# First units of a stage in two halves of 256 tokens, and the second mixer's values ahead of its keys and queries, in a kernel of two transformer blocks

## What is computed

```python
def token_mixing(x, mem, positions, w_in, b_in, pool_w, pool_scale, w_mem_kv, w_br, w_out):
    proj = jnp.einsum('bsd,de->bse', x, w_in) + b_in
    u_pool, q, k, v, iq, ik, iw, mq, gate_logits = jnp.split(proj, split_points, axis=-1)
    branches = (pool_branch(u_pool, pool_w, pool_scale),
                dsa_branch(q, k, v, iq, ik, iw, positions),   # rotary on q, k, iq, ik; top-128 by index score
                memory_branch(mq, mem, w_mem_kv))
    ...
def dsa_branch(...):
    rel = jax.nn.relu(jnp.einsum('bqhd,bsd->bqhs', iqb, ik) * (IDX_HEAD_DIM ** -0.5))
    score = jnp.einsum('bqhs,bqh->bqs', rel, iwb)
    ...
def second_block(...):
    for l in range(DEPTH):
        mix = token_mixing(...)
        x = layer_norm_2(DN_ALPHA_2 * x + mix, ln1_g[l], ln1_b[l])
        ffn = moe(...)                                        # 16 experts, two for each token
        x = layer_norm_2(DN_ALPHA_2 * x + ffn, ln2_g[l], ln2_b[l])
```

## Time and profile before

| | us |
|---|---|
| median of 3 runs | 3320.78 |
| lowest, highest | 3319.87, 3322.07 |
| profiled execution | 3319.54 |
| its span | 3317.7 |

### The profile page before, as it was taken

One profiled execution on the slowest core, in us unless ns is written; L12 is line 12 of the kernel. 1 busy time (PEld: TensorE's weight loads), 2 busy tenths in 40 slices (PEclk: granted clock), 3 DMA queues, 4 the chain that ended last, 5 costly groups with the idle time before them and its releaser, 6 DMA issues.

```text
span 3317.7 us, 44936 instructions
## 1 busy us (share of the span) xinstructions
PE 2972.4 (90%) x13284; PEld 2350.1 (71%) x13284; DVE 1805.6 (54%) x2681; ACT 1417.1 (43%) x2009; POOL 1100.6 (33%) x663
## 2 busy tenths in 40 slices
PE   5898999999879999999999977997599999969993
PEld 4666788876657888766777856885458777748883
DVE  3775444036655341346544157996556533169996
ACT  3525455225353552211344126885111443228882
POOL 2212344542122445444743521111336543601101
PEclk8998999999989999998999988998789999979996
DMA  3212233432122334322321337997212322349993
GB/s 111 64 32 83 76 95 95 166 91 67 33 71 81 96 95 153 109 71 58 101 67 48 105 141 289 411 411 283 79 58 82 88 64 64 111 161 401 411 410 132
DMA packets 373732, 461.46 MB, mean 139 GB/s; under 512 B 33396, under 2 KB 280262, under 8 KB 373512
## 3 DMA queue, kind: packets, MB, share of 16 engines
q1 hardware_dynamic: 353664, 392.05, 35.0%
q0 software_dynamic: 14976, 54.53, 4.3%
q10 hardware_dynamic: 4872, 12.26, 1.1%
HBM read 423.10 MB, written 35.65 MB: 138 GB/s over the span
## 4 chain that ended last, share of the span: by engine, by line
PE 48%; issue 33%; POOL 11%; DVE 5%; ACT 1%; DMA 1%; POOLq 0%; SPq 0%; DVEq 0%; ACTq 0%
POOL unit_lo L407 9%; PE bank L487 7%; PE bank L488 6%; PE bank L1997 4%; PE bank L2132 3%; PE bank L2133 3%; PE bank L2136 3%; PE bank L759 2%; PE bank L2146 2%; PE bank L2147 2%; PE bank L2150 2%; PE bank L2058 1%; PE bank L493 1%; PE bank L2074 1%; PE bank L494 1%
## 5 line engine op out<-in xcount | busy, mean ns | idle before, releaser
L407 POOL TENSOR_TENSOR unit_lo<-unit_raw,unit_hi 128x1024 fp32r<-128x1024 f32 (+1 forms) x176 | 422.5, 2402 | 893.0 <-ACT unit_hi L400 893.0
L487 PE MATMUL bank<-xT_hi,unit_hi 128*128 128x512 f32 x1680 | 692.3, 412 | 22.5 <-DVE xT_lo L661 9.9
L488 PE MATMUL bank<-xT_lo,unit_hi 128*128 128x512 f32 x1680 | 664.9, 396 | 0.0
L487 PEld LDWEIGHTS bank<-xT_hi,unit_hi 128*128 128x128 f32 x1680 | 322.4, 192 | 121.6 <-issue 44.6
L488 PEld LDWEIGHTS bank<-xT_lo,unit_hi 128*128 128x128 f32 x1680 | 322.1, 192 | 71.0 <-issue 7.7
L392 POOL TENSOR_TENSOR unit_lo<-unit_raw,unit_hi 128x1024 fp32r<-128x1024 f32 (+3 forms) x172 | 354.1, 2059 | 14.4
L400 ACT ACTIVATE unit_hi<-unit_raw 128x1024 fp32r<-128x1024 f32 (+1 forms) x176 | 184.9, 1052 | 406.6 <-PE bank L759 175.6
L390 POOL TENSOR_SCALAR unit_hi<-unit_raw 128x1024 fp32r<-128x1024 f32 (+3 forms) x172 | 159.6, 928 | 589.2 <-PE bank L1997 296.8
L759 PE MATMUL bank<-xT_hi,unit_lo 128*128 128x512 f32 x1040 | 256.9, 389 | 0.0
L472 DVE TENSOR_TENSOR wt_lo<-wt,wt_hi 128x1024 fp32r<-128x1024 f32 x192 | 229.2, 1222 | 32.1 <-ACT wt_hi L467 31.3
L472 DVE TENSOR_TENSOR xT_lo<-wt,xT_hi 128x1024 fp32r<-128x1024 f32 x192 | 234.5, 1223 | 12.3 <-ACT xT_hi L467 2.3
(11 more groups left out here) (514 smaller groups left out, 6471.4 us busy)
## 6 DMA issues: line engine op xcount, KB each, us to landing
wt<-in_w SPq DMA_DIRECT2D x384, 512.0 KB, 8.5
unit_raw<-in_w_in SPq DMA_DIRECT2D x276, 256.0 KB, 3.1
unit_raw<-in_w_ffn_up SPq DMA_DIRECT2D x176, 256.0 KB, 3.2
unit_raw<-in_w_ffn_down SPq DMA_DIRECT2D x88, 256.0 KB, 3.1
unit_raw<-in_w_out SPq DMA_DIRECT2D x64, 256.0 KB, 2.8
y_rows<-yb POOLq DMA_DIRECT2D x32, 512.0 KB, 7.3
y_rows<-zeros POOLq DMA_DIRECT2D x24, 512.0 KB, 5.2
unit_raw<-in_w_br SPq DMA_DIRECT2D x96, 128.0 KB, 2.2
```

The lines of the kernel that those rows point to most:

```text
L407: pool.eng.tensor_tensor(lo, raw, hi.bitcast(F32), SUB).then_inc(self.split, 1)
L487: pe.matmul(out, wh, xh, start=first, stop=False)
L488: pe.matmul(out, wh, xl, start=False, stop=False)
```

## The change

1. `norm_pe` is gone. `turned_rows` turns one tile. In `rows_products` tile i - 1 is turned behind the products of tile i; only the last tile is left for later.
2. `begun_units` starts the next stage: when tiles 0 and 1 have their low halves, the first unit is multiplied with 256 tokens (`first_half`); then the last tile is turned; then the second unit's first half; and when all low halves are there, the second halves of both. It stands at the start of the first and second block's layers and of the feed-forward part. The router's products are cut in two in the same way. To begin a layer, the last tile of the stage before is turned inside the next layer (hence the count 6 of `norm_tr`), and once more at the very end of the program.
3. DVE forms a tile's low half one tile later, between the variance and the inverse of the next but one; ACT alternates roots and copies.
4. In the second mixer the four value units come directly behind the index weights, tiles in the order 2, 3, 0, 1. DVE adds the value bias, loaded to all partitions, while it evicts them. Index scores are single: nine within the value units, the other fifteen before and behind units 5 to 12, over two banks. The memory rows are turned behind unit 15.

```diff
+        def first_half(T, j, half):
+            c = slice(half * 2 * P, half * 2 * P + 2 * P)
+            wh, wl = (w[j % SPLIT][:].rearrange("p (k c) -> p k c", c=P) for w in (ring.hi, ring.lo))
+            o = bank[j % SPLIT][:, c]
+            T.eng.wait_ge(ring.hi_made, ring.hi_is(T, j))
+            for k in range(KC):
+                two_of_three(T.eng, o, wh[:, k, :], xT_hi[:, k, c], xT_lo[:, k, c], k == 0)
+            T.eng.wait_ge(ring.split, ring.split_is(T, j))
+            for k in range(KC):
+                last = T.eng.matmul(o, wl[:, k, :], xT_hi[:, k, c], start=False, stop=k == KC - 1)
+            if half:
+                last.then_inc(ring.done, 1)
+        def begun_units(T, tile, first):
+            T.eng.wait_ge(norm_lo.sem, norm_lo.at(T, 2 * tile + 4))
+            first_half(T, first, 0)
+            turned_rows(T, tile + NT - 1)
+            first_half(T, first + 1, 0)
+            T.eng.wait_ge(norm_lo.sem, T.alone(norm_lo.at(T, 2 * (tile + NT))))
+            first_half(T, first, 1)
+            first_half(T, first + 1, 1)
...
# norm_v
-                    if i == NT - 1:
-                        low(0)
+                    if 0 < i < NT - 1:
+                        low(i - 1)
                     inverse(i)
                     finished(i)
-                for i in range(1, NT):
-                    low(i)
+                low(NT - 2)
+                low(NT - 1)
...
# rows_products
+                if i:
+                    turned_rows(T, tile + i - 1)
...
# tensor1, feed-forward part
-            norm_pe(T, 0)
-            T.eng.wait_ge(norm_lo.sem, T.alone(norm_lo.at(T, 8)))
-            with pe.Fori(0, FC // 2) as i:
+            begun_units(T, 0, U_UP)
+            for s in (2, 3):
+                chunk(T, ring, U_UP + s, bank[s])
+            T.eng.wait_ge(up_lo.sem, T.alone(up_lo.at(T, 1)))
+            with pe.Fori(1, FC // 2) as i:
...
# tensor2, the values
+            for j in range(4):
+                wh, wl = ring.weights(T, U2_V + j)
+                for x, i in enumerate(V_ORDER):
+                    if j == 0 and i < 2:
+                        T.eng.wait_ge(proj_ev.sem, proj_ev.at(T, 4 + i))
+                    for kk in range(2):
+                        k, cs, n = 2 * j + kk, slice(i * P, i * P + P), slice(kk * S, kk * S + S)
+                        last = triple(pe, bank[i][:], xT_hi[:, k, cs], xT_lo[:, k, cs], wh[:, n], wl[:, n], k == 0, k == 7)
+                    if x == NT - 1:
+                        last.then_inc(ring.done, 1)
+                    if j == 0 and x % 2:
+                        swap(3 + x // 2)
+                    elif j and x < NT - 1:
+                        index_score()
...
-                        pe.matmul(bank[i][:], ones[0:1, :], brow[:, 0:S], start=True, stop=False)
...
+            for c in range(5, 21):
+                if c < 8:
+                    T.eng.wait_ge(gv_ev.sem, gv_ev.at(T, c - 4))
+                else:
                     T.eng.wait_ge(proj_ev.sem, proj_ev.at(T, c - 2))
+                if c < ROPED:
+                    index_score()
                 chunk(T, ring, V_CH[c], bank[c % 3])
+                if 7 <= c < ROPED + 2:
+                    swap(c - 2)
+                if c < ROPED - 1:
+                    index_score()
+                if c == ROPED + 2:
+                    memory_turned()
...
# scalar2
-            act.dma_start(brow[:, 0:S], t["b_in_2"][bass.ds(l, 1), C_V:C_V + S]).then_inc(pl.sem, pl.up(A))
+            act.dma_start(v_bias, over(t["b_in_2"][bass.ds(l, 1), C_V:C_V + S], [P, S])).then_inc(pl.sem, pl.up(A))
...
# vector2
+            V.eng.wait_ge(ring.done, ring.products(V, U2_V + 3))
+            for i in (2, 0, 1, 3):
+                v.tensor_tensor(vv[:, i, :], bank[i][:], v_bias, ADD).then_inc(gv_ev.sem, gv_ev.up(V))
+            for c in range(5, ROPED):
+                accumulate()
+                if c >= 7:
+                    rope(c - 2)
+                if c < ROPED - 1:
+                    accumulate()
```

More of the change, by code:

```diff
@@ L729, in norm_a @@
-            high(0)
-            deviation(NT - 1)
-            for i in range(1, NT):
-                high(i)
[L734 to L741, removed]
+            if held:
+                deviation(0)
+                for i in range(NT - 1):
+                    high(i)
+                    deviation(i + 1)
+                high(NT - 1)
+                return
@@ new lines, in norm_a, with turned_rows @@
+            deviation(0)
+            deviation(1)
+            for i in range(NT):
+                if i + 2 < NT:
+                    deviation(i + 2)
+                high(i)
+        LAST = -NT
+        def turned_rows(T, tile):
+            T.eng.wait_ge(norm_z.sem, norm_z.at(T, tile + 1))
+            i = tile % NT
+            for x in range(2):
+                for k in range(4):
+                    last = T.eng.transpose(bank[2 * i + x][:, k * P:k * P + P],
+                                           h[:, i, (4 * x + k) * P:(4 * x + k + 1) * P], ident)
+                last.then_inc(norm_tr.sem, norm_tr.up(T))
@@ L847, in splits1, with rows_products @@
                     G.eng.dma_start(y_dram[rows, :].rearrange("p (x c) -> p x c", c=P), over(zeros[:].unsqueeze(1), [P, KC, P])).then_inc(y_zero.sem, y_zero.up(G))
-        def rows_products(T, first, count, held, x_hi, x_lo, made=None, late=None, order=None, ready=None):
+        def rows_products(T, tile, first, count, held, x_hi, x_lo, made=None, late=None, order=None, ready=None):
             def passes(k, i, hi, lo):
@@ L1914, in tensor2 @@
                     T.eng.wait_ge(proj_ev.sem, proj_ev.at(T, c - 2))
-                chunk(T, ring, V_CH[c], bank[c % 3])
-                if c == 4:
-                    wh, wl = (w[:, 0:64].rearrange("p (k c) -> p k c", k=KC) for w in ring.weights(T, U2_IW))
-                    for k in range(KC):
-                        last = triple(pe, bank[3][0:AH, :], wh[:, k, :], wl[:, k, :], xT_hi[:, k, :], xT_lo[:, k, :], k == 0, k == 7)
-                    last.then_inc(ring.done, 1)
+                if c >= SPLIT:
+                    chunk(T, ring, V_CH[c], bank[c % 3])
@@ L2201, in tensor2 @@
                 T.loop_end(NOV)
-            norm_pe(T, 1)
+            for i in range(NT - 1):
+                turned_rows(T, NT + i)
             for ended in (x_tr, h_tr):
@@ L2789, in tensor0 @@
             T.eng.wait_ge(tab_ev.sem, tab_ev.at(T, 4))
-            norm_pe(T, 0)
+            for i in range(NT - 1):
+                turned_rows(T, i)
         def scalar0(A):
@@ L2857, in _ @@
         def _(pe):
-            program(Lane(pe, began), "tensor")
+            T = Lane(pe, began)
+            program(T, "tensor")
+            turned_rows(T, 2 * NT - 1)
         @block.scalar
```

177 lines of the change are left out of this document (80 added, 97 removed).

## The result

The changed kernel took 3300.87 us in the median (3296.69 to 3302.16), against 3320.32 before: ratio 0.9940, 95% interval 0.9923 to 0.9957. It is faster by 19.5 us. The forecast was 3273, a gain of 47, and the time lies just above the range of 3252 to 3300. The profiled execution is the fastest of the four: 3296.69, span 3294.9, so against the earlier trace rows its gain is 22.8 us. These 22.8 are what can be laid out stage by stage.

The account below looks back on a forecast made before the run. PE, busy 90% of the span, bounds the kernel; time is won only where it waits or runs at half clock. Halves 29.7 + second mixer 18.4 = 48.1 us off 3319.5 gives 3271.4, median 1.2 above: 3273, range 3252 to 3300.

Parts of the forecast that it names:

- The halves: Half units begun before the last tile is normalised, at norms, layer starts and routers: 29.7 us gained (bounds 15 and 36).
- The feed-forward norm: Norm before the feed-forward stage, two layers: 6.4 us if the clock stays up, taken as 5.5 each, 11 together.
- the second block: Layer starts there: layer 0 gains 4.9 us, with 0.8 for the larger value-bias load; layer 1 gains 0.5 (-2 to +1.5).
- The second mixer: Its projection stage with values before keys and queries: 11 us gained in layer 0, 7.4 in layer 1, together 18.4.
- DVE's chain: Second mixer, last rotation to fourth pool: 46.7 us without a pause, moving only as the last rotation does.
- 125.7: Second mixer: us of PE's work, waits and switches from the third unit's start to the last rotation's product.
- the wait of 2.3 us: Second mixer, PE's wait for the fifth rotation: stays, but 2.3 us instead of 4.10.
- The fifth: Rival: second mixer gives its gain back, last rotation and last pool moved by 9 us a layer: 3291; chance 0.06.
- The first: Rival: clock drops at each new short wait, eight norms and the rotation, 31 us in all: 3304; chance 0.13.
- The second: Rival: second mixer's pools lose GpSimd lock waits, DVE's chain 8 us shorter a layer: 3257; chance 0.20.
- The third: Rival: halves don't start early, first two units' weights not split in time; only mixer's gain left: 3302; chance 0.03.
- fourth: Rival: single scores hold the clock at 0.50 through second mixer's values, keys and queries: slower, up to 3393; chance 0.03.

Follow-up runs that it names:

- x11: x6 with the nine scores among the second mixer's value units in pairs (2, 2, 2, 2, 1) instead of singly: 3246.55 us, ratio 0.9776.
- x6: Full change with x4's late scores, x3's 2 early ranking rounds, and separate semaphores for value bias and memory rows: 3251.56 us, ratio 0.9794.
- x7: x4 with the value bias again laid in by four PE products, loaded as one row of 2 KB; DVE only copies the values out: 3286.97 us.
- x3: Full change with 2 instead of 6 rounds of ranking ahead of the memory halves and pools, the other 4 later: 3279.87 us.
- x4_again: The same kernel as x4, measured once more beside later runs as their base: 3281.55 us.
- x1: Only the halves and the norms' new order, with the second mixer's order as before the change: 3279.37 us, ratio 0.988.
- x4: Full change with the nine scores among the value units begun two token tiles later: 3283.18 us.
- x10: x1 with the memory rows' loads given a semaphore of their own: 3275.88 us.
- x9: Full change with one score left where PE waits for the fifth rotation and the next two moved behind the following tiles: 3293.82 us.
- x2: Only the second mixer's new order, with norms and full first units as before the change: 3316.31 us, ratio 0.9989.

## Why the prediction was wrong

**The bound.** Right: PE's waits and half clock were the place where time could be won. x11 wins 74 us there.

**The halves.** Right. 28.3 us by the trace for 29.7. The feed-forward norm was computed at 6.4 and rounded down to 5.5; it gave 6.8 and 6.9, because the clock stayed at 1.00 behind the wait of 1.91. Part of this is luck: in x6, x7 and x11 the same wait of 1.9 us was followed by 3.4 us at half clock in both layers, in x3 and x4_again in one of them. The first norm gave 7.1 for 4.8. What fell short is the second block: 3.2 for 4.9 and -3.5 for 0.5. The step that failed among the halves is the loads. I had the value bias at 0.8 us; it costs 2.5 or more and 3.2 (x1 against the full change; 2.7 in layer 1 by x7). And in layer 1 I let the loads land about when PE asked, where PE stood still for 6.30 us. There ACT issues the first of them 2.8 us behind the end of its last copy. It does not do so in layer 0, but it did so in layer 1 before the change too (2.5 us), where PE came later; the forecast had no term for it, and no run shows what the gap is:

```profile
2335.68 1.08 ACT L724 ACTIVATE xT_hi<-bank 128x512 fp32r<-128x512 f32 x2 [7.81 <-PE bank L748]
2339.53 0.59 ACTq L2262 DMA_DIRECT2D vv<-in_b_in  x1
```

**The second mixer.** This is the part that failed: 18.4 forecast, -5.7 measured, which is 24 of the 28 us missed. Every link behind the last rotation held: DVE's chain 46.1 us for 46.7, the new wait 10.96 for 11 to 12, on ACT's copy of a memory-key unit, in both layers. The link in front failed, the term "125.7" for PE's work from the third unit to the last rotation's product: it took 138.0. The 12.3 us are in three parts. 8.5 are half clock (3.4 us of it behind the load wait and 13.7 behind the rotation wait, halved); I had placed the wait of 2.3 us between the 1.6 that do nothing and the 4.1 that halve the clock, and given it no clock at all. The kernel before contradicts that. Its wait of 2.33 us for a score in the earlier trace rows is followed by half clock from 1511.86 on, before the wait of 1.58 us that I counted as harmless is over. In layer 1 it stands alone, and 17.1 us at half clock follow it from 2474.42 on:

```profile
2474.04 1.73 PE L1907 MATMUL bank<-cosA,iq 64*128 64x512 f32 x2 [2.33 <-ACT up L2239]
```

Nor do waits of 1.6 us always do nothing: two of them in the first block are followed by 3.4 us at half clock (at 160.16 and 835.04), two in the second block by none (at 1844.10 and 2805.76). x4 took 8.9 and 8.3 us away in the two layers, wait and clock together. 0.3 are the wait itself, 2.62 for 2.3. The other 3.5 are the scores and the products between them: I read "1.22 for four records" as the price of four scores at full clock. It was a pair of scores, two records each, side by side, and at half clock. A single score costs 0.63 us like a pair, and the six value products behind each take 1.58 instead of 1.37. In x6, at full clock, the scores and what they cost the products beside them come to some 16 us; I had 12, so this is enough for the 3.5. (An estimate: 13.45 us between the starts of the scores and those of the products behind them, 0.2 us more at each of nine breaks among the value products and 0.1 at each of the eight others.) x11 gives the price the other way: 3.3 us for four breaks less.

**The rivals.** The fifth ("a wait upstream moves the last rotation and with it the last pool") is what happened, given 0.06. It was put down at 3291, and the measured time is 10 us above it: 5.7 because the mixer gave back more than its gain, 3.0 by the share of the median, and the rest mostly at the halves. It needed no mishap, only the wait that I had computed myself and whose clock I left out. The first (every short wait lowers the clock) was right at the rotation, at the loads and before the routers (waits of 1.9 us, 6.8 us at half clock behind each), and wrong in this trace at the other norms; as it was one rival for ten places, it could not come true in part. The second (DVE's pools become quicker once GpSimd stops) did not come, but was hardly put to the test: PE stood still from 1564.58, GpSimd split on until 1570.61, and only the last 4 us of the chain ran without it. The third and fourth did not come; x4 shows scattered scores at clock 1.00. The fourth had been put at 120 us more.

**The share of the median.** I set the median 1.2 us above the profiled execution. It lies 4.2 above it here. That and nothing of the mechanism is the last part of the miss.

## What to carry to other kernels

Where an engine off the critical path hangs on one instruction of the bounding engine, the place of that instruction is the forecast: sum the work ahead of it with the clock, and not beside it. Where a short wait stands in that sum, look for waits of its length in the trace and give the clock behind it a range. Separate the clock from the schedule before comparing two kernels: subtract half of the busy time at half clock from each stage. Here that showed at once that the new order had only turned work into waiting, and that a shorter chain (one constant, 21 us) and one wait less were wanted.

A wait that several loads share is as late as the largest of them. When the first user is moved forward, give each load its own semaphore.

## What was not expected of the hardware

- **The same wait can cost anything from nothing to 13.7 us at half clock, and what stands behind it is part of the reason.** A wait of 2.62 us was followed by 3.4 us at half clock in both layers where three tiles of value products stood behind the one score (x9). Where a score stood behind nearly every tile it was 13.7 us in five layers out of eight, 10.2 in two, and none in x2's second layer. With the wait gone the same scattered scores ran at 1.00 (x4). Before a feed-forward norm a wait of 1.9 us did nothing in the full change and brought 3.4 us at half clock in x6; before the routers it brought 6.8. No length of wait divides these cases, so no forecast of a single spell is safe. The Trainium skill, "TensorE: Matmul & The Clock Gate", section "HAM oscillation — how this bites in real kernels", tells of clock lost to waits between short runs of products; the traces agree that such spells begin at a wait, and x2 shows a wait without one.
- **Two products of 64 rows in different halves of the array cost one.** Even heads use rows 0 to 63 and odd heads 64 to 127: a pair of 256 columns takes 0.63 us from its start to the next value product, a single one 0.63. The Trainium skill, "TensorEngine Tiling (Array Packing)", section "Key Properties", says that different tiles of the array can work in parallel and that a change of mode drains the engine. The trace agrees with the first, and a drain would fit that the first value product behind a score lies 0.33 us ahead of the next where 0.23 is usual.
- **Much of a program's own spread is clock.** In x10 the same instructions took 190.1 us in one layer and 198.7 in the other, and half the difference of the busy time at half clock (18.4 us) is 9.2.
